# One weight pass for the first FFN of tiles 0 and 1, background casts of the second-half weights, second halves one tile later

## The reference

```python
h = h + 0.5 * swiglu(rms_norm(h, ffn1_norm[i]), ffn1_w_in[i], ffn1_w_out[i])   # D_FF = 2816
n = rms_norm(h, mix_norm[i])
gm_u, gm_v, sb_q, sb_k, sb_v = jnp.split(n @ w_mix_in[i], splits, axis=-1)
gm_out = chunked_gmlp(gelu(gm_u), gelu(gm_v), gmlp_v_norm[i], gmlp_w_s[i], gmlp_b[i])
sb_out = stick_breaking_attention(sb_q, sb_k, sb_v)       # 8 heads of 64, strictly causal
h = h + concat([gm_out, sb_out]) @ w_mix_out[i]
h = h + 0.5 * swiglu(rms_norm(h, ffn2_norm[i]), ffn2_w_in[i], ffn2_w_out[i])
gate = jax.nn.sigmoid(rms_norm(h, ple_norm[i]) @ ple_w_gate[i])
h = h + gate * (p[i] @ ple_w_proj[i])
return rms_norm(h, final_norm)
```

## Time and profile before

| | us |
|---|---|
| median of the three runs shown | 3547.43 (3542.98 to 3761.17) |
| profiled execution, its time | 3551.3 |
| profiled execution, span of its slowest core (core 6) | 3549.7 |
| spans of the eight cores | 3524.7 to 3549.7 |

### The profile page before, as it was taken

How to read it: one execution, slowest core, us unless ns; L and a number is a source line. 1 busy time by engine, 2 the same in 40 slices (tenths; PEclk the granted TensorE clock), 3 DMA queues, 4 the chain that set the end, 5 groups by cost and what they waited for, 6 DMA issues and landing times.

```text
span 3549.7 us, 53379 instructions; the slowest of 8 cores (3524.7 to 3549.7 us)
## 1 busy us (share of the span) xinstructions
PE 3047.5 (86%) x13632; PEld 1201.7 (34%) x13632; DVE 2083.9 (59%) x2219; ACT 1483.8 (42%) x2654; POOL 1636.8 (46%) x1186
## 2 busy tenths in 40 slices
PE   5779999676898989989898887998978979878898
PEld 2234333222343333333233332333323333223343
DVE  1124264333644677366773777847888758888632
ACT  2133344221534454434543445444454435454432
POOL 3314062254541656145561655616666427657521
PEclk9989999888999999999999998998999999989999
DMA  9995777898785767678586875877867968868653
GB/s 201 215 218 155 198 185 192 194 181 175 177 213 179 190 162 184 179 210 196 127 206 185 212 182 140 206 204 193 190 150 178 218 173 181 182 149 188 154 178 104
DMA packets 840768, 648.10 MB, mean 183 GB/s; under 512 B 591520, under 2 KB 609952, under 8 KB 839584
## 3 DMA queue, kind: packets, MB, share of 16 engines
q1 hardware_dynamic: 815424, 600.13, 66.2%
q0 software_dynamic: 25056, 44.58, 8.5%
HBM read 467.29 MB, written 83.36 MB: 155 GB/s over the span
## 4 chain that ended last, share of the span: by engine, by line
PE 55%; DMA 16%; DVE 12%; issue 6%; SPq 4%; ACT 4%; POOL 2%; DVEq 0%; POOLq 0%; ACTq 0%
PE bank L138 45%; DMA AT<-A 8%; PE zp L138 7%; DVE P L168 6%; DMA ring<-wpk 6%; PE bank L137 3%; SPq L177 3%; DVE hT L165 2%; DVE xnT L165 2%; DVE ef L157 2%; POOL A L157 2%; SPq L171 1%; ACT rr L148 1%; ACT sq L148 1%; DMA wscr<-ring 1%
## 5 line engine op out<-in xcount | busy, mean ns | idle before, releaser
L138 PE MATMUL bank<-xnT,ring 128*128 128x512 bf16 x6464 | 1593.3, 399 | 186.0 <-DVE xnT L165 78.5
L157 POOL TENSOR_TENSOR A<-P 128x1024 bf16<-128x1024 f32 (+2 forms) x576 | 1009.0, 1752 | 1251.5 <-DVE P L168 970.9
L168 DVE TENSOR_TENSOR_SCAN P<-zp,P,scanm 128x512 f32<-128x512 f32 (+3 forms) x1152 | 1358.7, 1189 | 76.4 <-ACT zp L148 15.2
L138 PEld LDWEIGHTS bank<-xnT,ring 128*128 128x128 bf16 x6464 | 616.8, 101 | 1064.0 <-issue 470.2
L148 ACT ACTIVATE zp<-zp 128x1024 f32<-128x1024 f32 (+2 forms) x576 | 541.8, 941 | 516.1 <-PE zp L138 515.4
L138 PE MATMUL bank<-hid,ring 128*128 128x512 bf16 x2640 | 615.6, 385 | 28.7 <-DMA ring<-wpk 25.5
L157 POOL TENSOR_TENSOR hid<-ef,up 128x512 bf16<-128x512 f32 x352 | 453.4, 1288 | 389.2 <-ACT up L154 201.5
L157 DVE TENSOR_TENSOR ef<-ef,bank 128x512 f32<-128x512 f32 x388 | 265.4, 684 | 572.9 <-ACT ef L148 509.9
L138 PEld LDWEIGHTS bank<-hid,ring 128*128 128x128 bf16 x2640 | 245.2, 99 | 356.2 <-issue 95.7
L138 PE MATMUL zp<-kvb,qT 64*128 64x512 bf16 x896 | 228.7, 395 | 127.0 <-DVE P L168 125.2
L148 ACT ACTIVATE sq<-hT 128x512 bf16<-128x512 f32 x320 | 189.7, 625 | 302.5 <-DVE hT L165 287.6
(11 more groups left out here) (72 smaller groups left out, 1280.8 us busy)
## 6 DMA issues: line engine op xcount, KB each, us to landing
ring<-wscr SPq DMA_DIRECT2D x1106, 256.0 KB, 3.8
ring<-wpk POOLq DMA_DIRECT2D x158, 256.0 KB, 11.9
wscr<-ring SPq DMA_DIRECT2D x158, 256.0 KB, 9.0
kvb<-kvscr SPq DMA_DIRECT2D x112, 256.0 KB, 3.6
ring<-wscr SPq DMA_DIRECT2D x112, 192.0 KB, 3.6
hT<-xT SPq DMA_DIRECT2D x32, 512.0 KB, 11.8
outT<-hT SPq DMA_DIRECT2D x32, 512.0 KB, 3.1
hscr<-hT SPq DMA_DIRECT2D x28, 512.0 KB, 4.2
```

Of the source, the lines that this page charges most:

```text
L138: return lambda e: e.matmul(out, lhsT, rhs, start=start, stop=stop)
L157: return lambda e: e.tensor_tensor(out, in0, in1, op)
L168: return lambda e: e.tensor_tensor_scan(out, in0, in1, init, op0, op1)
```

## The change

Five things change.

- `joint_front` runs the first FFN of tiles 0 and 1 together: each weight unit is taken once and used for both. The hidden values, scaled inputs and squares of tile 1 lie in buffers that attention uses later (`P`, `A`, `AT`). Stage 0 then has no F.
- The 78 units of the second FFN, `pg` and `pp` (`converted`) are no longer cast into the ring. `convert` issues on GpSimd a DMA that casts from `wpk` straight into `wscr`, after every second dense step of stages 0 to 2, with at most six under way (`cv_res`). Their use in B is a plain load.
- For the units that are still cast into the ring, the store into `wscr` is issued when the unit after it is taken, no longer right behind the cast.
- B comes one tile later: stage t from 3 on has B of tile t - 3, and stage 7 has B of tiles 4, 5 and 6. The use of the three `h` buffers changes to fit; the third load in stage 7 waits until the first B's output is on its way (`late_load`).
- In `mix_front_gen` the gMLP products come ahead of the k and v projections, and k and v wait in the order for the last product of attention that reads `kvcur` (`kv_free`).

```diff
+NCV = 6
+CVSTEP = 2
...
+    def converted(u):
+        return u[0] in ("pp", "pg") or u[0] in ("in", "out") and u[1] == 1
...
+    hid1 = salloc("hid1", [128, NFF, T], BF16, at=step_off)[0]
+    xn1 = salloc("xn1", [128, 8, T], BF16, at=at_off)[0]
+    sq1 = salloc("sqs1", [128, 8, T], BF16, at=at_off + 8 * T * 2)[0]
...
+        def norm_scale(bp, sqs=None):
...
-                S.op("pe", f_mm(ssb.ap, ones_bf, sqb[k][:, :], k == 0, k == 7), reads=[sq_res[k], R_const], writes=ssb.res)
+                S.op("pe", f_mm(ssb.ap, ones_bf, sqs[k][0], k == 0, k == 7), reads=sqs[k][1] + [R_const], writes=ssb.res)
...
+            while late_load:
+                load_stage(late_load.pop())
...
-            return 0 if t == 0 else 1 if t % 2 else 2
+            return (0, 1, 2)[t] if t < 3 else (2, 0)[t % 2]
...
+        def joint_front(bp):
+            step_res = P_res + A_res
+            tiles = ((hid, scr_res, [], xnT, xnT_res, []),
+                     (hid1, hid1_res, step_res, xn1, xn1_res, AT_res[0]))
...
+            for k in range(8):
+                square(0, k)
+            norm(0, 0, bp)
+            for k in range(8):
+                square1(k)
+            r = scale1()
+            for k in range(8):
+                norm_apply(0, 1, k, r, xn1[:, k, :], xn1_res[k])
+            n = 0
+            for c in range(NFF):
+                gu = []
+                for half in range(2):
+                    w = rg.get(("in", 0, c, half))
+                    for t in range(2):
+                        xs, xr, al = tiles[t][3:6]
+                        bk = bp.next()
+                        for k in range(8):
+                            S.op("pe", f_mm(bk.ap, w.ap[:, k * 128:(k + 1) * 128], xs[:, k, :], k == 0, k == 7),
+                                 reads=w.res + [xr[k]] + al, writes=bk.res)
+                        gu.append(bk)
+                for t in range(2):
+                    hd, hr = tiles[t][0:2]
+                    bg, bu = gu[t], gu[2 + t]
+                    ef = efb[t][:, :]
+                    er = [ef_res[t]]
+                    S.op("act", f_act(ef, bg.ap, AF.Sigmoid), reads=bg.res, writes=er)
+                    S.op("dve", f_tt(ef, ef, bg.ap, ALU.mult), reads=er + bg.res, writes=er)
+                    S.op("act", f_acopy(upb[t][:, :], bu.ap), reads=bu.res, writes=[up_res[t]])
+                    S.op("pool", f_tt(hd[:, c, :], ef, upb[t][:, :], ALU.mult), reads=er + [up_res[t]], writes=[hr[c]])
+            for j in range(8):
+                by = [bp.next(), bp.next()]
+                for piece in range(3):
+                    w = rg.get(("out", 0, j, piece))
+                    for t in range(2):
+                        hd, hr, al = tiles[t][0:3]
+                        for c in range(piece * 8, min(piece * 8 + 8, NFF)):
+                            ci = c - piece * 8
+                            S.op("pe", f_mm(by[t].ap, w.ap[:, ci * 128:(ci + 1) * 128], hd[:, c, :], c == 0, c == NFF - 1),
+                                 reads=w.res + [hr[c]] + al, writes=by[t].res)
...
+            norm(1, 0, bp)
+            return scale1()
...
-                square(nxt, 2 * qc)
-                square(nxt, 2 * qc + 1)
+                if nxt is not None:
+                    square(nxt, 2 * qc)
+                    square(nxt, 2 * qc + 1)
...
-            pre_r.append(norm_scale(bp))
+            if nxt is not None:
+                pre_r.append(norm_scale(bp))
...
-            for kc in range(4):
-                w = rg.get(("mi_k", kc))
-                bk = bp.next()
-                proj8(w, xnT, xnT_res, bk)
-                emit_copy("act", kvcur[:, kc, 0:512], bk.ap, bk.res, [kvcur_res[kc]])
...
-            if ti + 1 < NT:
-                S.op("sp", f_dma(kvscr[ti, :, :], kvcur[:, :, :].rearrange("p h c -> p (h c)")), reads=kvcur_res, writes=[kvscr_res[ti]], dma="ks")
...
             for h in range(4):
...
+            while not kv_free[0]:
+                yield
+            for kc in range(4):
+                w = rg.get(("mi_k", kc))
+                bk = bp.next()
+                proj8(w, xnT, xnT_res, bk)
+                emit_copy("act", kvcur[:, kc, 0:512], bk.ap, bk.res, [kvcur_res[kc]])
+                yield
...
+            if ti + 1 < NT:
+                S.op("sp", f_dma(kvscr[ti, :, :], kvcur[:, :, :].rearrange("p h c -> p (h c)")), reads=kvcur_res, writes=[kvscr_res[ti]], dma="ks")
...
+            kv_free[0] = False
...
+                if hp == 3 and c == ti:
+                    kv_free[0] = True
...
-                if ti >= 2:
-                    st.append(("B", ti - 2, 0))
-                st.append(("F", ti + 1, hbuf(ti + 1)))
+                if ti >= 3:
+                    st.append(("B", ti - 3, 1))
+                if ti >= 1:
+                    st.append(("F", ti + 1, hbuf(ti + 1)))
             else:
-                st.append(("B", NT - 3, 0))
-                st.append(("B", NT - 2, hbuf(NT - 2)))
+                st.append(("B", NT - 4, 1))
+                st.append(("B", NT - 3, 2))
+                st.append(("B", NT - 2, 1))
...
+        def convert():
+            i = conv_n[0]
+            if i < len(conv_todo):
+                u = conv_todo[i]
+                nco = unit_cols(u)
+                S.op("pool", f_dma(wscr[uidx[u], :, 0:nco], wpk_d[uidx[u], :, 0:nco]),
+                     writes=[wscr_res[uidx[u]], cv_res[i % NCV]], dma="cv%d" % (i % NCV))
+                conv_n[0] += 1
+
         def dense_gen(ti):
+            n = 0
+            for _ in dense_parts(ti):
+                n += 1
+                if ti < 3 and n % CVSTEP == 0:
+                    convert()
+                yield
+            if ti == 2:
+                while conv_n[0] < len(conv_todo):
+                    convert()
...
                         after = st[i + 1][2]
-                        load_stage(st[i + 1])
+                        if i == 0:
+                            load_stage(st[i + 1])
+                        else:
+                            late_load.append(st[i + 1])
                     for _ in back_gen(t, hb, side, after, pre_r.pop()):
                         yield
+            if ti == 0:
+                for k in range(8):
+                    norm_apply(1, 1, k, r1, xnT[:, k, :], xnT_res[k])
+                yield
...
-        for k in range(8):
-            square(0, k)
         load_x(1)
-        run(front_gen(0, allbanks))
-        run(mix_front_gen(0, hbuf(1), allbanks))
+        r1 = joint_front(allbanks)
+        run(mix_front_gen(0, None, allbanks))
...
-                if first_occ[L]:
+                if first_occ[L] and not converted(uu):
                     S.op("pool", f_dma(ring[sl][:, 0:ncols], wpk_d[ui, :, 0:ncols]), writes=[ring_res[sl]], dma="g%d" % sl)
-                    if NT > 1:
-                        S.op("sp", f_dma(wscr[ui, :, 0:ncols], ring[sl][:, 0:ncols]), reads=[ring_res[sl]], writes=[wscr_res[ui]], dma="w%d" % sl)
+                    self.unsaved[L] = (sl, ui, ncols)
...
+            if idx - 1 in self.unsaved:
+                sl, ui, ncols = self.unsaved.pop(idx - 1)
+                S.op("sp", f_dma(wscr[ui, :, 0:ncols], ring[sl][:, 0:ncols]), reads=[ring_res[sl]], writes=[wscr_res[ui]], dma="w%d" % sl)
```

48 lines of the change are left out of this document (36 added, 12 removed).

## The result

The changed kernel takes 3608.07 us (median of 3 runs, 3596.88 to 3772.75) against 3547.43: the ratio is 1.0149, interval 1.0124 to 1.0174. It is slower by 1.5%, where I had forecast 3418 and a range of 3380 to 3485. The profiled execution took 3596.88 us, its span is 3595.3 (core 3).

What follows compares the result with a forecast made beforehand. TensorE was taken as the bound, its idle time of 502 us of 3550 as winnable. Start 326, stages 90 + 215 + 222 + 1754 + 11 + 639, last B 163: 3420, 3418 us on the median; range 3380 to 3485.

Steps and rivals of the forecast that it cites:

- Stage 0, 90 forecast: Stage 0, attention 0 and tile 1's projections alone: 85 us plus 5 for casts ahead on GpSimd, ending at 416.
- I take 1.75, near the cast: Background converts: each DRAM-to-DRAM cast takes 1.75 us of all 16 DMA engines, giving 215 us for stage 1.
- high bound of 2.52: Background converts: upper bound per convert, cast plus store, 2.52 us, which made stage 1 249 us.
- first rival: Converts at the high bound, transposes held up behind big pieces: stage 1 249, stage 0 another 11; 3463 us; chance 0.14.
- attention is not what ends stages 0 and 1: Stages 0 and 1: the argument given against the rival at 3463 us, in which transposes are held up behind converts.
- three signs that I had named for being wrong: GpSimd waits for converts, weights come late in stage 1, or stage 7 grows by a whole B.
- Stage 2, 222 forecast: Stage 2 without B: stage 1 plus one attention row, taken as 18 us more, 222 against 476.
- Nothing waits there: Stage 2: DMA need is 0.75 x 222 + 19 x 1.75 = 200 us, so nothing waits.
- The 80 us of stage 2 before: Stage 2 before, 476 us, 80 over stage 3: laid to SyncE's 111 us waits for casts, holding up attention transposes.
- the 11 I had allowed for: Stages 3 to 6: gMLP products ahead of k and v wait for `gvn`, 2.7 us each, 11 in all.
- a stall moved to GpSimd: Rival: converts landing later than 27 us after issue stall GpSimd instead of SyncE; 71 us, so 3489; chance 0.04.
- fourth rival: Slower than before: DRAM-to-DRAM casts much dearer than both parts; at 4.5 us per convert, 3610; chance 0.05.

## Why the prediction was wrong, step by step

**The start.** Right: the sums behind the joint FFN begin at 273.54 in the kernel after (forecast 273), attention 0 begins at 326.73 (forecast 326):

```profile
273.54 1.89 PE L140 MATMUL zp<-sq,ones_bf 128*128 128x512 bf16 x8
...
326.73 0.34 PE L140 MATMUL zp<-kvcur,qT 64*128 64x128 bf16 x4 [0.89 <-ACT kvcur L156]
```

**Stage 0, 90 forecast, 131 measured.** Without converts it lasts 112 (328 to 440), so 19 are the converts. The rest is one term. k, v and the output projection took the 30 us that I had put on them. What stands ahead of them was to take 55 (45 of VectorE's work, 8 for the last block, 2 of begin) and 5 more for the casts; without converts it took 82. VectorE's busy time was right, but the stage is not bound by it: VectorE sat idle in between, for scores that come through ScalarE's sigmoid. The two parts of the stage without converts, and VectorE's wait from 326 to 412 (13.3 us of it from ahead of the stage):

```profile
328.00:410.00 82.00, 46.45 (x173) 16.68 (x176) 44.35 (x55) 39.89 (x74) 22.41 (x20) 0.71 0.48 121
410.00:440.00 30.00, 29.57 (x133) 13.36 (x136) 5.53 (x8) 4.96 (x10) 2.11 (x4) 0.94 0.74 189
```
```profile
DVE P L170 <- ACT zp L150: 38.9, 6, 13.3
```

TensorE makes the scores, in turns with projections, at a granted clock of 0.71 there; how much of VectorE's wait is owed to that was not taken apart. With the converts, TensorE's waits for transposes grow from 12.7 us to

```profile
PE bank L139 <- DMA AT<-A: 32.4, 3, 23.8
```

That the coupled half transposes bind stage 0 fell too where no convert stands beside it (550 against 545); beside converts, undoing them gives 10 (446 against 456).

**Converts, the step that failed.** "I take 1.75, near the cast": the convert's own packets measured 1.7, but the DMA work of the stage rose by 2.4 per convert, near the high bound of 2.52 (by the rows cast plus store is 1.81 + 0.77 = 2.58, which makes that bound of the stage 252, not 249). By that the stage needed 255, not 215: about the first rival's 249. Then "attention is not what ends stages 0 and 1" was wrong as well: late transposes, and the loads queued behind them, held stage 1 up for another 48 us, of which the half transposes gave 31 back. The first rival had price and direction right and less than half of the size: 45 us in stages 0 and 1, where 88 and 19 were measured. It had no term for the chain, and the big pieces that it blamed are worth 12. Two of the three signs that I had named for being wrong came: GpSimd waited for converts (20.1 us) and weights came late (35.5).

**Stage 2, 222 forecast.** Without converts and with the half transposes apart it is 219 to 227; with converts alone gone, 246; as changed, 273. "Nothing waits there" at 0.75 + 19 x 1.75 / 222 of DMA share was the failed step: the stage had a share of 0.79, and TensorE still waited for transposes. A share below 1.0 over a stage doesn't say that nothing waits in it.

**The 80 us of stage 2 before.** I put them on SyncE's waits and counted them as won. They are for the most part what 78 casts cost at first use, 81 us in stage 3 without converts; SyncE's part was about 17. The converts then cost 132, more than the casts that they replaced.

**Stages 3 to 6.** 20 us over the forecast. The `gvn` wait is 3.6 us a stage as read from the earlier trace rows, but putting the products back gives 35 in these stages, three times the 11 I had allowed for; less busy time of TensorE is part of it, the rest stays open.

**Stage 7 and the last B.** Right in kind: 620 and 159 (forecast 639 and 163, bounds from 627). The term that was off is TensorE's busy time: 546 us, not 424 + 144 = 568, at a granted clock of 0.95 where the stage had 0.92 and the last B 0.93. Its busy share, 0.881, is near the 0.888 taken, and its idle time, 74 us, near the forecast's 71. The scan waits fell from 54.6, as forecast, while those for scaled inputs rose from 9.1; the two are now

```profile
PE zp L140 <- DVE P L170: 29.8, 32, 3.2
PE bank L140 <- DVE xnT L167: 15.9, 9, 3.3
```

**The range.** The case that decided was neither at 4.5 us per convert nor a stall moved to GpSimd (20.1 us of waits for converts in stage 1; the converts landed a median 6.8 us after their issue and at most 22.6, not 27). That 3610, the fourth rival's time, stands next to the measured 3608 is chance. What came was rival one, with a chain that I had argued away, and 42 us to the end of stage 0 beside it.

## What to carry to other kernels

Price background DMA work by what it adds to all queues, not by its own packets, and only count it as hidden where the engines have room for that. Look at the share in short stretches: the 0.84 of stage 1 was 1.14 while the last converts ran and 0.44 behind them, and beside a chain of small transfers that wait for one another that was not free. When a stall sits behind a wait, take the wait away alone before counting its cure as a gain: here it was worth 17 of 80 us. And look for waits that come from tracking a buffer too coarsely; two halves written apart and tracked as one cost 60 us in the kernel before and about twice that in the kernel after.

## What the runs showed of the hardware that I had not expected

A transpose's issue on SyncE is not a fixed cost: 44 of them took 61.8 us in stage 1 of the kernel before (longest 5.64), 122.6 after (longest 32.78), and 99.3 with two converts under way (longest 10.44). While one is being issued, all of SyncE's queue stands. Packets of one queue get longer beside another's: nearly the same bytes, 40 MB, took 148 us of the engines alone and 178 beside converts. And TensorE's granted clock adds to the stalls: 0.84 in stage 1 and 0.74 in stage 0 of the kernel after, where it waits, 0.97 and 0.95 in these stages of the kernel before.
